# Encoder step on one core: expert dots placed earlier, one-hots shared with ScalarE, later weights in half-row blocks

## The chip, the cores and the metric

One core of one Trainium2 chip runs the whole program. The metric is the device time of one execution in microseconds (us), the median of several runs. The profile shows one execution; its span is counted from the first to the last recorded instruction. MB are 10^6 bytes unless a size in KB stands beside.

## The reference, cut to what matters

640 tokens of width D = 2048 (four tiles of 128 prompt tokens, one tile of 8 x 16 sample tokens) pass one layer, all in float32:

```python
z = (rmsnorm(x) * (1 + sc1) + sh1) @ w_in            # value, gate, q, k, v
y = concat(conv_module(z), band_attention(q, k, v))  # 1024 + 1024 channels
x = x + g1 * (y @ w_out)
h = rmsnorm(x) * (1 + sc2) + sh2                     # PEER retrieval on h
s = (h @ w_pq) . sub_keys                            # 8 heads x 2 x 128 scores
# per head: top 16 of each half, 256 sums, top 16 of those -> 128 experts a token
act = gelu(einsum('td,ted->te', h, u_experts[eidx])) # the "dots"
x = x + g2 * einsum('te,ted->td', softmax(tv) * act, v_experts[eidx])
return rmsnorm(x) * final_g                          # and the new caches
```

There are 16384 experts of 2048 values each, in `u_experts` and in `v_experts`.

## The kernel before, in words

**Tokens.** Tiles 0 and 1 ("first tiles", X, TX = 2) and tiles 2 to 4 ("later tiles", Y, TY = 3; tile 4 holds the sample tokens) are taken through the dense layers one after the other. The first tiles go first, so that their expert retrieval can run beside the dense layers of the later ones.

**Dots.** Each of the 5 x 128 = 640 steps takes one expert per token. POOL (`gather`, L637 to L640) fetches 128 rows of 8 KB, 1 MB, by an indirect DMA into one of NU = 4 buffers `ux`; VectorE (`step`, L1724) multiplies them with h and sums. Dot n belongs to tile n // 128. Behind a dot VectorE runs one piece of `choose` (L1551), the search for the picks of the head after next, 18 pieces a head. `steps(k)` in the VectorE program places k dots: 112 after the first tiles' queries (L1748), 1.5 a head in the later tiles' attention (L1797, L1800), 28 among the residual additions of w_out (L1813), all others after it (L1818). A waiting dot holds up everything behind it on VectorE.

**Weights.** SP loads them in blocks of 256 columns, all 16 row blocks, 2 MB, so 1 KB rows (`load`, L322, `load_pq`, L383). For the later tiles two of the four slots of R0 are in turn, and each load waits until TensorE has done the block two before it. TensorE takes q and k columns with `project` (L743), v rows with `values_part` (L782), w_out with `project_out` (L871), and w_pq with `key_queries` (L893), whose scores ScalarE copies to `SY`. SP saves them (L497), loads tile 2's again as `Sc` (L499); choices 16 and later read them there. ScalarE's copies of v (`keep_values`, L1094) wait for stores of v, which SP issues (`values_out`, L407) between loads; `k_cache(0)` comes after all of them.

**Attention of the later tiles.** For each of 16 heads VectorE runs `head_mask`, `head_max`, `steps(1)`, `head_norm`, then in odd heads `steps(1)`; TensorE runs `scores` (L949 to L955), `weigh` and `turn_weights`. `scores(h)` waits for the maximum of head h-1.

**V side for the prompt tiles, in two pairs of tiles.** `turn_picks` transposes a tile's indices and weights, ScalarE copies them (`copy_turned`, L1269). `one_hots(n)` (L1639) builds four tokens' one-hot rows of both indices on VectorE in one of four slots: L1648 the second index, L1649 the first times the weight. `scatter_tokens` multiplies them on TensorE (L1029) into a 128 x 128 weight matrix a token, and ScalarE copies it into `W` (`keep_W`, L1276). 64 such groups make a pair. `dense(pair)` (L1033) then streams all of `v_experts` in 128 pieces of 1 MB through TensorE (L1040), 16 matmul records a piece, into all eight banks. The one-hots of a pair are built in one go, `burst` (L1699): the first one when dot 256 is due, with 36 pieces of `choose` between; the second when dot DRAIN * TOPK = 33 * 16 = 528 is due, behind `drain` (L1667), which empties the banks:

```python
if n == DRAIN * TOPK:
    drain()
    burst(64, None)
```

One-hot slots share memory with two of the four slots of the pieces, and `W` with the other two, so no piece arrives during a burst.

**End.** Tile 4's V side is 128 gathered picks, added by L1829. Then `first_pair_out` (tiles 0 and 1), tile 4, and `last_pair_out` run one after another (L1832 to L1838), each with `norm_rows` (L1653); SP stores the rows, and loads x1 of the last pair once the first pair is stored. SP issues `finals` (the first pair's inputs and gates) after piece 84 of the second pair.

**Orders.** Nothing is planned at run time: each engine's program is a fixed list, joined by semaphores.

Of the kernel before, what the change touches and what calls it, by code (L numbers as in the profile page):

```python
# [5 lines left out]
def hybrid_encoder_step(nc, ins, outs):  # L6
# [12 lines left out]
    ALU = mybir.AluOpType  # L19
# [28 lines left out]
    DRAIN = 33  # L48
# [8 lines left out]
    with ctx:  # L57
# [64 lines left out]
        vst = VS[:, 0:1024].rearrange("p (b n) -> p b n", b=4)  # L122
        ost = rb(29696, 2048).rearrange("p (b n) -> p b n", b=2)
# [68 lines left out]
        fin = tk(16)  # L192
        assert ms_at[0] <= 3776 and tk_at[0] <= tk_end and late_at[0] <= 3776
# [47 lines left out]
        s_vsty = [sem(f"later_v_stored_{i}") for i in range(4)]  # L241
# [17 lines left out]
        q_done, q_read, s_s, s_se = sem("q2_done"), sem("q2_read"), sem("key_scores"), sem("key_scores_read")  # L259
        w_q = [sem(f"w_pq_{i}") for i in range(2)]  # L260
# [7 lines left out]
        tr_done, tr_read = sem("picks_turned"), sem("turned_copied")  # L268
        oh_rdy, oh_used, w_read = sem("onehots"), sem("onehots_used"), sem("W_copied")
# [4 lines left out]
        s_h2in, s_Sin = sem("h2_in"), sem("keyscores_in")  # L274
        s_fin, s_fin2, s_x1l = sem("final_in"), sem("final_in_sample"), sem("x1_last_in")
# [45 lines left out]
        def _(sp):  # L321
# [72 lines left out]
            for m in range(12):  # L394
                if m < 2:
                    sp.wait_ge(q_done, 14 + 2 * m)
                elif m < 10:
                    sp.wait_ge(z_done, 40 + 2 * (m - 1))
                else:
                    sp.wait_ge(z_done, 56 + 3 * (m - 9))  # L400
                load("w_in", m % 2, (2 + m // 4) * CC + (m % 4) * BW)
                if 8 <= m < 11:
                    i = m - 4
                    sp.wait_ge(s_oE, i + 1)
                    sp.dma_start(kvo["k", 0][i - 2] if i < 6 else kvo["k", 1], ost[:, i % 2]).then_inc(s_osty[i % 2], 16)

                def values_out(j):  # L407
                    for t in range(TX, T):
                        v = j * TY + t - TX
                        sp.wait_ge(z_free, 2 + 56 + v + 1)  # L410
                        dst = kvo["v", 0][t] if t < TP else kvo["v", 1]
                        sp.dma_start(dst[:, j * BW:(j + 1) * BW], vst[:, v % 4]).then_inc(s_vsty[v % 4], 16)

                if m >= 10:
                    values_out(m - 10)
# [1452 lines left out]
```

## Time and profile before

| | us |
|---|---|
| median of 3 runs | 4321.93 (4309.65 to 4325.44) |
| profiled execution, time | 4329.54 |
| profiled execution, span | 4327.7 |
| TensorE busy | 3614.2 (84%) |
| VectorE busy | 2841.8 (66%) |
| GpSimd (POOL) busy | 1160.0 (27%) |
| ScalarE busy | 337.1 (8%) |
| moved by DMA | 1402.75 MB, mean 324 GB/s |

How to read it: busy is the time in which an instruction was recorded on the engine. PEld is TensorE's weight load, which overlaps the multiplies. PEclk is the clock granted to TensorE as a share of full speed. The DMA share is the mean busy share of 16 DMA engines; it can come out a little over 1. Idle time of an engine costs nothing where another one sets the end.

### The profile page before, as it was taken

The numbers are of one execution on the slowest core, as the hardware profiler recorded it, in microseconds if no ns is written. First come the engines' busy times: TensorE is split into PE (matmuls) and PEld (weight loads), VectorE is DVE, ScalarE is ACT, GpSimd is POOL, SyncE is SP. The second block draws the span as 40 slices with busy tenths as digits, with TensorE's granted clock in tenths as the row PEclk, the third lists the DMA queues.
The fourth block names the chain that finished last, engine by engine and source line by source line (L and its number), as shares of the span: only waits on it lengthen the run. The fifth ranks groups of instructions, "written<-read, shape, count | busy, mean of one in ns | idle before, by whom it ended". The sixth has DMA issues, their size and how long they took to land.

```text
span 4327.7 us, 36032 instructions
## 1 busy us (share of the span) xinstructions
PE 3614.2 (84%) x13071; PEld 2135.0 (49%) x13071; DVE 2841.8 (66%) x5321; ACT 337.1 (8%) x763; POOL 1160.0 (27%) x862
## 2 busy tenths in 40 slices
PE   4699899997887989891689999999526899996995
PEld 0466577875456777550534444444215344442442
DVE  2138861148883755887987766676899766664657
ACT  1100013110001400100200000000002000000000
POOL 1100001015661112564043222222641422222221
PEclk8899999998997999895899999999769999998997
DMA  9977834459997879998189999999972999999996
GB/s 350 206 255 243 261 104 150 151 205 401 398 403 251 278 263 334 342 388 326 40 352 418 421 421 407 422 420 421 387 270 84 421 422 419 419 422 395 421 418 256
DMA packets 406612, 1402.75 MB, mean 324 GB/s; under 512 B 22512, under 2 KB 246456, under 8 KB 268933
## 3 DMA queue, kind: packets, MB, share of 16 engines
q0 software_dynamic: 116784, 831.77, 48.5%
q1 hardware_dynamic: 289088, 564.69, 35.8%
q10 hardware_dynamic: 576, 4.19, 0.2%
q8 instruction: 91, 1.49, 0.1%
q14 instruction: 73, 0.60, 0.0%
HBM read 1370.26 MB, written 31.81 MB: 324 GB/s over the span
## 4 chain that ended last, share of the span: by engine, by line
DMA 45%; PE 28%; DVE 12%; issue 10%; POOL 3%; SPq 1%; ACT 1%; another core or an unknown queue 0%; DVEq 0%; POOLq 0%; ACTq 0%
DMA R<-in_u_experts,MS 28%; PE bank L743 13%; DMA R<-in_v_experts,MS 9%; PE bank L871 6%; DVE R L1649 3%; POOL R L639 3%; PE bank L782 3%; DMA R<-in_w_in 3%; DMA R<-in_w_ada 2%; DVE R L1648 2%; DVE R L1829 2%; PE bank L697 1%; PE bank L674 1%; DVE RB L1435 1%; PE bank L955 1%
## 5 line engine op out<-in xcount | busy, mean ns | idle before, releaser
L639 POOL DMA_INDIRECT R<-in_u_experts,MS x640 | 979.7, 1531 | 1859.8 <-DVE MS L1724 1568.7
L1724 DVE CUSTOM_DVE_ANT_0 R<-R 128x2048 f32<-128x2048 f32 x384 | 880.8, 2294 | 406.8 <-DMA R<-in_u_experts,MS 386.7
L1040 PE MATMUL bank<-R,RB 128*128 128x512 f32 x2304 | 1019.0, 600 | 73.4 <-DMA R<-in_v_experts 73.2
L743 PE MATMUL bank<-RB,R 128*128 128x256 f32 (+1 forms) x3072 | 862.8, 443 | 96.4 <-DMA R<-in_w_pq 45.0
L1040 PE MATMUL bank<-RB 128*128 128x512 f32 x1792 | 778.2, 592 | 0.0
L743 PEld LDWEIGHTS bank<-RB,R 128*128 128x128 f32 x3072 | 593.8, 195 | 351.8 <-issue 51.5
L1040 PEld LDWEIGHTS bank<-R,RB 128*128 128x128 f32 x2304 | 440.0, 192 | 642.4 <-issue 544.6
L1724 DVE CUSTOM_DVE_ANT_0 R<-R,RB 128x2048 f32<-128x2048 f32 x256 | 585.9, 2289 | 123.8 <-DMA R<-in_u_experts,MS 122.3
L1040 PEld LDWEIGHTS bank<-RB 128*128 128x128 f32 x1792 | 340.5, 190 | 428.6 <-issue 428.6
L1829 DVE SCALAR_TENSOR_TENSOR R<-R,MS 128x2048 f32<-128x2048 f32 x128 | 301.5, 2355 | 211.1 <-DMA R<-in_v_experts,MS 210.6
L871 PE MATMUL bank<-R,RB 128*128 128x256 f32 x1280 | 279.7, 382 | 10.4 <-DMA R<-in_w_out 9.3
L871 PEld LDWEIGHTS bank<-R,RB 128*128 128x128 f32 x1280 | 244.9, 192 | 44.8 <-DMA R<-in_w_out 9.7
L639 POOL DMA_INDIRECT R<-in_v_experts,MS x128 | 130.8, 1022 | 392.0 <-DVE R L1829 362.8
L1029 PE MATMUL bank<-R 128*128 128x128 f32 x1024 | 164.1, 309 | 83.7 <-DVE R L1649 83.3
L674 PE MATMUL bank<-MS,RB 128*128 128x128 f32 (+4 forms) x497 | 83.4, 320 | 176.8 <-DVE RB L1637 92.3
L1029 PEld LDWEIGHTS bank<-R 128*128 128x128 f32 x1024 | 138.9, 211 | 109.3 <-DVE R L1649 109.0
L1649 DVE TENSOR_SCALAR R<-MS 128x128 f32<-128x128 f32 x512 | 176.3, 344 | 0.0
L1435 DVE SCALAR_TENSOR_TENSOR RB<-RB,MS 128x512 f32<-128x512 f32 x240 | 175.8, 732 | 0.0
L674 PEld LDWEIGHTS bank<-MS,RB 128*128 128x128 f32 (+4 forms) x497 | 66.3, 173 | 190.7 <-DVE RB L1637 92.9
L782 PE MATMUL bank<-R,RB 128*128 128x256 f32 x640 | 142.9, 386 | 14.1 <-DMA R<-in_w_in 10.3
L1354 DVE TENSOR_TENSOR RB<-bank,RB 9x256 f32<-9x256 f32 x128 | 53.5, 418 | 153.3 <-PE bank L697 149.3
L1648 DVE TENSOR_SCALAR R<-MS 128x128 f32<-128x128 f32 x512 | 145.1, 283 | 1.6 <-ACT MS L1269 1.5
(282 smaller groups left out, 1912.9 us busy)
## 6 DMA issues: line engine op xcount, KB each, us to landing
R<-in_v_experts SPq DMA_DIRECT2D x144, 1024.0 KB, 9.1
RB<-in_v_experts SPq DMA_DIRECT2D x112, 1024.0 KB, 9.1
R<-in_w_ada SPq DMA_DIRECT2D x48, 2048.0 KB, 13.2
R<-in_w_in SPq DMA_DIRECT2D x32, 2048.0 KB, 18.5
R<-in_w_out SPq DMA_DIRECT2D x16, 2048.0 KB, 9.2
R<-in_w_pq SPq DMA_DIRECT2D x16, 2048.0 KB, 21.4
R<-in_u_experts,MS POOLq DMA_INDIRECT x640, 10.9
RB<-in_x_prompt POOLq DMA_DIRECT2D x6, 1024.0 KB, 16.6
```

The lines of the kernel that those rows point to most:

```text
L639: pool.indirect_dma_start(dst, None, table, bass.IndirectOffsetOnAxis(ap=expert[T_ % 2][:, c:c + 1], axis=0)).then_inc(signal, 16)
L674: return pe.transpose(out, in_, ident[0:k, 0:k])
L743: m = pe.matmul(PB[2 * par + i][:, 0:src.shape[-1]], w, src[:, k], start=(k == 0), stop=(k == KT - 1))
L782: m_ = pe.matmul(PB[2 * (n % 2)][:, 0:BW], src[:, k, t * P:(t + 1) * P], ring[:, j, k, :], start=(k == 0), stop=(k == KT - 1))
L871: m = pe.matmul(PB[v % 4][:, 0:BW], src[:, k, t * P:(t + 1) * P], ring[:, j % 2, k, :], start=(k == 0), stop=(k == KT - 1))
L1029: m = pe.matmul(PB[n % 4][:, k * P:(k + 1) * P], oneh[n % 4][:, 1, k], oneh[n % 4][:, 0, k], start=True, stop=True)
L1040: x = pe.matmul(PB[4 * h + q][:, :], W[:, i, h * P:(h + 1) * P], vring[slot][:, q * PW:(q + 1) * PW], start=(i == 0), stop=(i == NKEY - 1))
L1435: ch.mark(STT(out=oP, in0=iP, scalar=w, in1=oP, op0=ALU.mult, op1=ALU.add))
L1648: TS(oneh[n % 4][:, 1, k], iota_row, turned[t % 2][:, 1, c:c + 1], None, ALU.is_equal)
L1649: m = TS(oneh[n % 4][:, 0, k], iota_row, turned[t % 2][:, 0, c:c + 1], turned[t % 2][:, 2, c:c + 1], ALU.is_equal, ALU.mult)
L1724: V.tensor_tensor_reduce(u, u, x1[t] if t < TX else h2c, 1.0, 0.0, ALU.mult, ALU.add, dots[t % 2][:, h * TOPK + s:h * TOPK + s + 1]).then_ ...
L1829: STT(out=acc, in0=ux[p % NU], scalar=weight[TP][:, p:p + 1], in1=acc, op0=ALU.mult, op1=ALU.add).then_inc(v_used, 1)
```

## The change

- More dots early: `steps(124)` for 112, three dots a head for 1.5, four after each of twelve w_out residuals.
- The later tiles' w_in, w_out and w_pq come in half-row blocks: 8 of 16 row blocks and 512 columns, 2 MB again, 2 KB rows; sums over both halves stay open in several banks. v and w_out rows are taken 512 columns at a time, v through two staging buffers of 512. The k-cache load moves up.
- ScalarE builds the second index's one-hots of odd groups (distance to the index by Abs, then Relu of 1 minus it).
- DRAIN becomes dot 492. The third tile's groups are built between dots 494 to 511, the fourth tile's in one go when dot 512 is due; ScalarE's program is put in that order.
- The first pair's output runs in nine parts behind V picks 80 to 88; the last rows' squares move to ScalarE.

```diff
-    DRAIN = 33
+    DRAIN = 492
@@ SP
+            def load_half(n, name, at, signal):
+                if n >= 2:
+                    if n % 2 == 0:
+                        sp.wait_ge(y_used, n // 2)
+                    else:
+                        second_half_used(n // 2 - 1)
+                sp.dma_start(wide[:, n % 2], wv[name][:, (n % 2) * 8:(n % 2) * 8 + 8, at:at + PW]).then_inc(signal[n % 2], 16)
...
+            for n in range(12):
+                if n < 2:
+                    sp.wait_ge(q_done, 14 + 2 * n)
+                load_half(n, "w_in", (2 + n // 4) * CC + (n // 2 % 2) * PW, w_in_s)
+                if n == 1:
+                    k_cache(0)
...
+            values_out(0)
+            for n in range(12, 14):
+                load_half(n, "w_out", 0, w_in_s)
+            values_out(1)
...
@@ TensorE
+            for b in range(4):
+                for half in range(2):
+                    weights_in(half)
+                    for c in range(4):
+                        n = 40 + 4 * b + c
+                        if half == 0:
+                            pe.wait_ge(z_free, n - 1)
+                        m = half_columns(hTY, half, c, c)
+                        if half:
+                            m.then_inc(z_done, 1)
+                        elif c == 3:
+                            m.then_inc(y_used, 1)
...
                     pe.wait_ge(oh_rdy, n + 1)
+                    if n % 2:
+                        pe.wait_ge(oh_act, n // 2 + 1)
...
-                for t in (2 * pair, 2 * pair + 1):
-                    turn_picks(t)
-                for t in (2 * pair, 2 * pair + 1):
-                    scatter_tokens(t)
+                turn_picks(2 * pair)
+                if pair == 0:
+                    turn_picks(1)
+                scatter_tokens(2 * pair)
+                if pair:
+                    turn_picks(3)
+                scatter_tokens(2 * pair + 1)
                 dense(pair)
@@ ScalarE
+            for v in range(2 * TY):
+                act.wait_ge(z_done, 56 + v + 1)
+                if v >= 2:
+                    act.wait_ge(s_vsty[v % 2], 16 * (v // 2))
+                A(vstY[:, v % 2], PB[v][:, :], ACT.Copy).then_inc(z_free, 1)
...
+            def distances(n):
+                t, q = divmod(n, P // 4)
+                for k in range(4):
+                    m = A(oneh[n % 4][:, 1, k], iota_row, ACT.Abs, scale=-1.0, bias=turned[t % 2][:, 1, 4 * q + k:4 * q + k + 1])
+                m.then_inc(oh_abs, 1)
+
+            def second_rows(n):
+                act.wait_ge(oh_abs, n // 2 + 1)
+                A(oneh[n % 4][:, 1], oneh[n % 4][:, 1], ACT.Relu, scale=-1.0, bias=ones).then_inc(oh_act, 1)
+
             def keep_W(t):
...
+                for n in range(n0, n1):
+                    at = (t % 2) * P + 4 * (n - n0)
+                    ahead = n % 2 == 0 and n + 3 < n1
+                    if ahead:
+                        if n:
+                            act.wait_ge(oh_used, n)
+                        distances(n + 3)
                     act.wait_ge(oh_used, n + 1)
                     A(W[:, :, at:at + 4], PB[n % 4][:, :].rearrange("p (t i) -> p i t", t=4), ACT.Copy).then_inc(w_read, 1)
+                    if ahead:
+                        second_rows(n + 3)
...
+            def last_squares(n, x, junk, at):
+                act.wait_ge(f_x, n + 1)
+                A(junk, x, ACT.Square, accum_out=fin[:, at:at + 1]).then_inc(s_sq, 1)
...
+            row_sqrt(0, 0, 2)
+            last_squares(0, x1r[2], acc, 10)
+            last_squares(1, x1r[0], accd[0], 0)
+            last_squares(2, x1r[1], accd[1], 1)
+            row_sqrt(1, 10, 1)
+            row_sqrt(2, 0, 2)
@@ VectorE
-                    TS(oneh[n % 4][:, 1, k], iota_row, turned[t % 2][:, 1, c:c + 1], None, ALU.is_equal)
+                    if n % 2 == 0:
+                        TS(oneh[n % 4][:, 1, k], iota_row, turned[t % 2][:, 1, c:c + 1], None, ALU.is_equal)
...
-                if n == DRAIN * TOPK:
+                if n == DRAIN:
                     drain()
-                    burst(64, None)
+                if n == TP * P:
+                    for k in range(4):
+                        weigh_picks(3, k)
+                    for q in range(P // 4):
+                        one_hots(3 * (P // 4) + q)
...
+                if DRAIN + 2 <= n < TP * P:
+                    per = TP * P - DRAIN - 2
+                    m = n - DRAIN - 2
+                    for q in range(m * 32 // per, (m + 1) * 32 // per):
+                        one_hots(2 * (P // 4) + q)
...
-            steps(112)
+            steps(124)
...
                 steps(1)
                 head_norm(h)
-                if h % 2:
-                    steps(1)
+                steps(2)
...
-            for v in range(8 * TY):
+            for v in range(4 * TY):
...
+                steps(4)
...
+                if 80 <= p < 89:
+                    first_pair_out(p - 80)
+
+            last_rows()
```

`last_rows` does tile 4's and the last pair's additions, then the three row scales and outputs; `row_scale` is the small middle part of the old `norm_rows`.

## Rows read from the trace of the kernel before

**Rows 1.** Stretches: length, busy PE, PEld, DVE, ACT, POOL, then PEclk, DMA share, GB/s.

```profile
945.00:1752.00 807.00, 682.32 (x3091) 530.37 (x3089) 548.63 (x1068) 107.26 (x290) 298.24 (x165) 0.89 0.90 329
1388.00:1542.00 154.00, 146.91 (x946) 115.81 (x946) 113.63 (x337) 64.95 (x190) 23.01 (x24) 0.84 0.76 253
1752.00:1955.00 203.00, 183.86 (x608) 111.69 (x608) 170.08 (x267) 15.53 (x32) 135.79 (x64) 0.95 0.99 383
2048.00:2181.00 133.00, 89.29 (x515) 75.58 (x515) 132.97 (x595) 38.70 (x65) 3.82 (x4) 0.85 0.11 41
2181.00:3085.00 904.00, 886.73 (x2047) 389.54 (x2048) 635.66 (x1027) 6.06 (x7) 262.18 (x230) 0.99 1.01 416
3085.00:3207.00 122.00, 0.61 (x2) 0.00 (x0) 111.66 (x184) 0.31 (x1) 98.01 (x42) 0.52 0.95 363
3207.00:3332.00 125.00, 77.20 (x518) 64.94 (x518) 123.45 (x525) 39.33 (x67) 1.55 (x2) 0.95 0.14 49
3332.00:4273.00 941.00, 887.05 (x2037) 389.04 (x2038) 596.01 (x552) 4.00 (x5) 261.59 (x236) 0.97 1.01 414
4273.00:4328.00 55.00, 4.92 (x12) 1.90 (x10) 48.40 (x49) 0.61 (x3) 0.00 (x0) 0.58 0.33 133
```

**Rows 2.** The same view for line 1724 alone; two records are one dot.

```profile
1388.00:1542.00 154.00, 55.05 (x48) 0.84 0.76 253
2181.00:3085.00 904.00, 529.48 (x459) 0.99 1.01 416
3085.00:3207.00 122.00, 94.22 (x84) 0.52 0.95 363
```

**Rows 3.** Timeline of VectorE at the first head and the first w_out residual.

```profile
1387.69 0.29 DVE L1765 CUSTOM_DVE_ANT_0 RB<-bank,MS 128x128 f32<-128x128 f32 x1 [8.14 <-PE bank L955]
...
1562.78 0.42 DVE L1509 TENSOR_TENSOR MS<-bank,RB 128x256 f32<-128x256 f32 x1 [31.62 <-DMA RB<-mod_scratch]
```

**Rows 4.** DMA view of 1026 to 1320 us (three rows), then of 0 to 80.

```profile
q0 software_dynamic: 12712, 92.61, 77.3%
q1 hardware_dynamic: 23942, 25.40, 25.5%
...
R<-in_w_in SPq DMA_DIRECT2D x12, 2048.0 KB, 27.5
...
q1 hardware_dynamic: 9639, 19.46, 72.7%
```

**Rows 5.** Timeline of SP's queue after the later queries.

```profile
1955.61 1.70 SPq L497 DMA_DIRECT2D keyscore_scratch<-RB  x3
1978.22 0.32 SPq L499 DMA_DIRECT2D R<-keyscore_scratch  x1
```

**Rows 6.** Timeline in the bursts, one group of TensorE in each, builds on VectorE.

```profile
2054.84 2.07 PE L1029 MATMUL bank<-R 128*128 128x128 f32 x8 [0.25 <-DVE R L1649]
...
3222.83 0.28 DVE L1648 TENSOR_SCALAR R<-MS 128x128 f32<-128x128 f32 x1
...
3222.97 1.16 PE L1029 MATMUL bank<-R 128*128 128x128 f32 x8 [0.65 <-DVE R L1649]
3223.02 0.34 DVE L1649 TENSOR_SCALAR R<-MS 128x128 f32<-128x128 f32 x1
3223.28 0.28 DVE L1648 TENSOR_SCALAR R<-MS 128x128 f32<-128x128 f32 x1
```

**Rows 7.** ScalarE's groups by form: busy us and mean ns, then the idle time.

```profile
L1276 ACT ACTIVATE RB<-bank 128x512 f32<-128x512 f32 x128 | 76.1, 597 | 171.9 <-PE bank L1029 165.1 <-DMA acc_scratch<-RB 6.8
...
L1246 ACT ACTIVATE RB<-RB,MS 128x512 f32<-128x512 f32 x16 | 11.4, 712 | 0.0
...
L1142 ACT ACTIVATE RB<-RB,MS 128x128 f32<-128x128 f32 x16 | 6.4, 400 | 12.0 <-DVE MS L1488 12.0
...
L1219 ACT ACTIVATE RB<-bank 128x128 f32<-128x128 f32 x16 | 4.6, 285 | 0.0
```

**Rows 8.** Timeline of VectorE at the last output rows.

```profile
4318.60 4.62 DVE L1665 SCALAR_TENSOR_TENSOR RB<-RB,MS 128x2048 f32<-128x2048 f32 x2
```

More of the change, by code:

```diff
@@ L192, in hybrid_encoder_step @@
         fin = tk(16)
+        ones = fin[:, 15:16]
         assert ms_at[0] <= 3776 and tk_at[0] <= tk_end and late_at[0] <= 3776
@@ L391, in _ @@
                 load_pq(m)
[L394 to L415, printed above, removed]
-            values_out(2)
-            values_out(3)
-            for j in range(2):
-                sp.wait_ge(z_done, 56 + 3 * (j + 3))
-                load("w_out", j, j * BW)
             def k_cache(hp):
@@ L434, in values @@
                         sp.wait_ge(s_vst[i], 16 * 2)
+                    for i in range(2):
                         sp.wait_ge(s_vsty[i], 16 * 3)
@@ L466, in _ @@
             sp.dma_start(n2Y, rows(ins["norm2_g"].tensor, [[0, P]], D)).then_inc(s_n2, 16)
-            for j in range(2, 8):
-                sp.wait_ge(o_done, 16 + 3 * (j - 1))
-                load("w_out", j % 2, j * BW)
-                if j == 4:
+            for n in range(14, 20):
+                load_half(n, "w_out", (n - 12) // 2 * PW, w_in_s)
+                if n == 16:
                     sp.wait_ge(s_A2, 3)
@@ L665, in _ @@
             pool.wait_ge(s_osty[1], 16)
-            for i in range(4):
+            for i in range(2):
                 pool.wait_ge(s_vsty[i], 16 * 3)
@@ L921, in _, with half_columns, half_rows @@
             pe.wait_ge(s_se, 16)
-            columns(40, hTY, 8)
+            def half_columns(src, half, c, bank):
+                for i in range(8):
+                    m = pe.matmul(PB[bank][:, 0:NY], wide[:, half, i, c * P:(c + 1) * P], src[:, 8 * half + i],
+                                  start=(half + i == 0), stop=(half + i == 8))
+                return m
+            def half_rows(src, half, t, bank):
+                for i in range(8):
+                    m = pe.matmul(PB[bank][:, :], src[:, 8 * half + i, t * P:(t + 1) * P], wide[:, half, i, :],
+                                  start=(half + i == 0), stop=(half + i == 8))
+                return m
+            for b in range(4):
[10 more added lines that the diff above has]
+                            m.then_inc(y_used, 1)
             for i in range(4, 7):
@@ L1011, in _ @@
             pe.wait_ge(s_h2E, 4 * T)
-            key_queries(1, h2TY, TY)
+            for b in range(4):
+                for half in range(2):
+                    pe.wait_ge(w_q[half], 16 * (4 + b + 1))
+                    for c in range(4):
+                        n = 4 * b + c
+                        if half == 0 and n >= 4:
+                            pe.wait_ge(q_read, 16 + n - 3)
+                        m = half_columns(h2TY, half, c, c)
+                        if half:
+                            m.then_inc(q_done, 1)
+                            if n >= 1:
+                                key_scores(1, n - 1, TY)
+                        elif c == 3:
+                            m.then_inc(y_used, 1)
+            key_scores(1, 15, TY)
             def turn_picks(t):
```

193 lines of the change are left out of this document (118 added, 75 removed).

## The prediction

> **What bounds the kernel now.** I read the windows view first, to cut the span into stretches, then the groups by form and the releasers. [rows 1] show four kinds of stretch. While the later tiles (2 to 4) are projected, 945 to 1752 us, the DMA share averages 0.90 and VectorE is busy 549 of 807 us: dots (L1724) fill gaps between other work. In the two dense stretches, 2181 to 3085 and 3332 to 4273, TensorE (887 of 904 us, 887 of 941) and the DMA engines (1.01) are both full. Between them TensorE has nothing to multiply for 122 us (0.61 us busy) while VectorE runs on to dot 528, where the old DRAIN lies. And in both one-hot bursts, 2048 to 2181 and 3207 to 3332, DMA falls to 0.11 and 0.14 while VectorE is full. The last 55 us are VectorE alone. So the reader should see two things to gain: expert rows moved while a queue is idle, and VectorE time in bursts and tail.
>
> The chip moves 1 MB (1.05 MB decimal) for a dot, a V pick and a dense piece alike. The second dense stretch has 112 dots, 128 picks and 128 pieces in 941 us: 2.56 us each. With free queues a dot costs VectorE 2.9 us, choice included (84 records are 42 dots in 122 us [rows 2]; busy 94.2/42 = 2.24 is the dot, 0.66 the choice).
>
> **Step 1, more dots early (56).** Before, 112 + 24 + 28 = 164 dots are done ahead of the later query projection; after, 124 + 48 + 48 = 220.
> - First projections: 12 dots x 2.9 = 35 us on VectorE after 1326, so it is free for the heads at 1361. Before, it then waited until 1387.7 for the first maximum [rows 3]; the k-cache load is now issued earlier, and the first head needs some 7 us of TensorE. Start 1375: -13. The six later v tiles have banks of their own, but only two staging buffers; v 5's copy waits for v 3's store, which SP issues behind the last w_out load: some 20 us, under the same 35.
> - Heads: before, VectorE did 1.5 dots a head, TensorE 147 of 154 us. Its other work is 113.6 - 55.1 - 24 x 0.66 = 43 us, 2.7 a head. After: 2.7 + 3 x 2.9 = 11.4 us, with its gaps 12.2, times 16 = 195 against 154: +41. VectorE, not TensorE, becomes the bound.
> - w_out: TensorE work is unchanged. VectorE starts 21 us late, waiting for g1 [rows 3], then 12 x (4 x 2.9 + 1.4) + 4.5 = 161 us, then norms and turn, 23 us: from 1575 this chain gives 1780.
> - DMA sets a later end: 807 x 0.90 = 726 share-us are needed already; 56 x 1.05 MB at 0.411 MB a us (416 GB/s by 1.01) add 143, so 945 + 869 = 1814, or 1805 at the share of 1.01 of the dense stretches. I take 1812 for the key queries' start, against 1752: **+60**.
>
> **Step 2, half-row blocks.** They change rows from 1 to 2 KB. In the w_in stretch the 1 KB rows moved 25.40 MB in 25.5% of 294 us, 339 GB/s of their own time; the 2 KB rows of w_ada moved 19.46 MB in 72.7% of 80 us, 335 [rows 4]. So no queue time is gained: 0, bounded by -18 us if 58 MB ran as fast as the gathers (92.6 MB in 77.3%: 407) and 0. What may change is who waits: w_in lands after a median 27.5 us [rows 4] against 20.8 us of TensorE a block. The DMA total above is unchanged by that. On SP the k-cache load (0.5 MB, 1 us of queue time) now stands behind the second half-block, and each half waits for its own half of TensorE's work, 20.5 us before its successor is needed; POOL's queue only loses two waits at its end.
>
> **Step 3, key queries and first burst.** Only 36 dots remain (before 92), done by about 1812 - 10 + 105 = 1907. The queries need TensorE 184 us [rows 1], 203 with their waits. With the gathers gone half way I take 190: 2002. Before, this was hidden under dots; now the burst waits for it. Then the key scores are saved (1955.6 to 1978.2 before, under gathers [rows 5]) and reloaded before choice 16 can run. Bounds 14 (alone) and 32 us (as before); the queues are idle, so 17: 2019.
> ScalarE takes second one-hots of odd groups. A VectorE pair of builds is 0.45 us [rows 6], a group 4 x 0.455 = 1.81, now 1.05 in odd ones: a pair of groups 3.63 -> 2.86. The old burst was 133 us = 64 x 1.81 + 17 (36 choices, handshake); the new 32 x 2.86 + 17 = 108. ScalarE's pair is four Abs, a Relu and two copies. Nearest rows [rows 7]: 0.285 us for 128 columns from a bank, 0.400 for an Exp with sum between buffers, 0.597 for a 512-column copy. So 4 x 0.285 + 3 x 0.597 = 2.93, at most 4 x 0.400 + 3 x 0.712 = 3.74; I take 3.0 because neither new operation sums. It hides in 108/32 = 3.4; at 3.74 the burst is 120. Dense starts at 2127 against 2181: **-54**.
> The Trainium skill (ScalarE: Activation LUTs, Rules for kernel authors) advises VectorE for such operations and budgets about 0.3 us an ACTIVATE plus 0.83 ns an element; that gives 4 x 0.41 + 3 x 0.72 = 3.8 us, the burst 122, a sum 20 us worse with the second one. The trace's 0.285 and 0.597 us are below it, so it stays out of the sum.
>
> **Step 4, first dense stretch.** TensorE's 904 us stay. In them 459/2 = 229 dots ran; after 256 that reaches 485. DRAIN at 492 needs 7 more, 20 us, in place of 122: **-102**.
>
> **Step 5, builds between dots.** Drain 5 us; 20 dots x 2.9 = 58; 32 builds, 16 x 2.86 = 46; handshakes with gelu and the turn 6; the other 32 builds 46 + 3. Sum 164 against 125: **+39**. TensorE's 1.16 us a group and ScalarE's 3 a pair hide in 5.8 us a pair here. POOL was busy 98 us for 42 gathers in [rows 1], 2.3 each, against some 5.4 a step now; that hides too.
>
> **Step 6, second dense stretch.** 128 dots instead of 112: 16 x 2.56 = **+41**. The nine parts of the first pair's output, 2.3 us each, stand beside picks, an operation of the form and size of the last output rows (2.3 us each [rows 8]), that come every 4 us or so: 2.56 us a MB, shared with the pieces: 9 x (4.6 - 4.0) = 5 us late, part made up: **+4**. Its loads are issued at piece 84, some 250 us before pick 80.
>
> **Step 7, tail.** Of 55 us, the first pair took 20 (two each of four 2.3 us operations and the scale). Left: 4.6 sample, 9.6 for eight drains and two adds, 2.5 waiting for ScalarE's squares and root behind them, 3.2 scales, 7 outputs, 4.5 store [rows 8] = 31: **-24**.
>
> Sum: -54 - 102 + 39 + 41 + 4 - 24 = -96 us (the +60 lies inside the -54). The profiled execution had a span of 4327.7 and took 4329.5; it gives 4233. It stands 0.18% over the median 4321.9, so I forecast 4225.
>
> **Rivals.**
> *A, more is gained.* Each weight load lands within the 20.8 us of a block instead of 27.5, so TensorE no longer waits: key start 1800 (-12), queries 180 (-10), the scores' trip 14 (-3), no lag at the picks (-4): 4196. For it: 1 KB rows get only a quarter of the queue time beside the gathers. Against: what they gain the dots lose. The Trainium skill (DMA: Bandwidth & Descriptors, Queues, rings and completion order) says that an engine takes turns between queues packet by packet, so longer rows could raise their share; no row here decides it.
> *B, little is gained.* The early dots cost full price and collide: key start 1845 (+33), the scores' trip 32 (+15), ScalarE at 3.74 in both bursts (+12 + 11): 4296. For it: the queues are 0.90 full before the key queries already, and 0.76 among the heads.
> *C, slower: ScalarE and TensorE in turns.* keep_W runs Abs, waits for a group, copies, runs Relu, and the next copy waits again. If nothing overlaps, a pair is 1.6 + 2.07 + 0.6 + 0.7 + 2.07 + 0.6 = 7.6 us (2.07: a group of TensorE at its lower clock, 1.16 at the higher [rows 6]). First burst 243 (+135), third tile's builds 122 (+73), second's +18: 4451. It decides from 5.4 us a pair: over the 3.4 that VectorE leaves, 48 pairs then cost 96, the whole gain (5.9 us: 0.5% slower). Against it: distances are made three groups ahead, with four slots.
>
> **How the numbers follow.** Forecast 0.60; A 0.15; B 0.17; C 0.08. The forecast's own bounds are +-35 us (burst 12, trip 15, key start 15, lag 10). The range runs from 4150, below A for the 18 us of step 2 and step 1's unsure overlap, to 4305, above B; it leaves out C and edges. About 0.5%, 22 us, is what a measurement of this kernel can tell. Faster by more: forecast, A and half of B, 0.83; same: half of B, 0.09; slower: C, 0.08.
>
> **What would show it.** Right: the first query matmul for later tiles near 1812 with the heads 195 us long; over 70 us without dots ahead of the first burst, which is about 108 long with ScalarE at 3.0 us a pair; dense from 2127; TensorE without dense pieces for 184 us instead of 247 between the dense stretches; no first-pair work after the last pick. Wrong: w_in waits gone and a key start before 1790 (A), dots spaced over 3.3 us after 1326 (B), or VectorE waiting for TensorE in every build (C).

## Result and profile after

The changed kernel takes 4225.9 us, median of 4 runs (4220.1 to 4230.9), against 4319.3 for the kernel before (4 runs): a ratio of 0.978, 95% interval 0.9765 to 0.9797. The forecast was 4225. The profiled execution has a span of 4223.9 us, 104 less than 4327.7; the sum in the prediction gave 96 less. A second set of runs, on the chip of e10 to e12, gave 0.975 (0.9734 to 0.9771). So a difference of some 0.3%, 12 us, between experiments from different sets can be noise in what follows. One run of e3 (6147 us) and one of e9 (9608 us) lie far above all others and are left out of the medians.

The page after, in its rows on DMA and totals (40 equal slices):

```profile
DMA  9977834459999999993199999999948999999996
...
DMA packets 377072, 1402.68 MB, mean 332 GB/s; under 512 B 22416, under 2 KB 187480, under 8 KB 239397
```

The windows view of the changed kernel; columns and stretches as in [rows 1], with the heads as the second row and the later key queries as the third:

```profile
945.00:1792.00 847.00, 697.40 (x2489) 427.81 (x2488) 690.54 (x1276) 103.81 (x279) 387.40 (x220) 0.86 1.00 381
1373.00:1565.00 192.00, 174.33 (x954) 134.53 (x953) 177.66 (x442) 65.01 (x190) 73.55 (x48) 0.72 0.98 354
1792.00:1982.00 190.00, 183.04 (x619) 112.21 (x617) 67.00 (x68) 18.68 (x37) 55.66 (x29) 0.97 0.61 235
2007.00:2112.00 105.00, 74.75 (x508) 65.10 (x506) 105.00 (x463) 91.82 (x223) 3.76 (x4) 0.95 0.12 42
2116.00:3024.00 908.00, 887.53 (x2048) 389.30 (x2047) 640.55 (x1036) 4.78 (x6) 265.94 (x233) 0.99 1.01 417
3031.00:3190.00 159.00, 94.32 (x518) 84.45 (x518) 152.86 (x488) 95.39 (x229) 23.61 (x22) 0.71 0.50 177
3190.00:4131.00 941.00, 888.11 (x2048) 389.94 (x2048) 610.65 (x617) 3.69 (x6) 278.96 (x236) 0.98 1.01 415
4194.00:4224.00 30.00, 0.00 (x0) 0.00 (x0) 22.54 (x27) 6.31 (x8) 0.00 (x0) 0.50 0.25 105
```

Read it beside [rows 1]. The stretch of the later tiles has gone from a DMA share of 0.90 to 1.00: the early dots do fill the queues. But the key queries, where the share was 0.99, now show 0.61, and VectorE is busy for only 67 of their 190 us. The two dense stretches are what they were (TensorE 887 and 888 us busy, share 1.01). The ledger against before is:

| place | before | after | change of its length | forecast |
|---|---|---|---|---|
| start to first dense piece | 2181.2 | 2115.8 | -65 | -54 |
| first dense piece to drain | 1026.2 | 915.0 | -111 | -102 |
| drain to second dense piece | 124.8 | 159.8 | +35 | +39 |
| second dense piece to last pick's end | 940.6 | 1003.2 | +63 | +45 |
| tail | 54.6 | 30.1 | -25 | -24 |

Every stretch lies within 18 us of its forecast, and the sum within 8. In the second profile of the changed kernel (e13) the first dense piece comes at 2126.5 and not at 2115.8, so the first row is good to some 10 us. Where its 65 us come from is another matter. VectorE stands still in the middle of the key queries; its timeline around dot 248, and under it SP's:

```profile
1878.61 2.29 DVE L1850 CUSTOM_DVE_ANT_0 R<-R,RB 128x2048 f32<-128x2048 f32 x1 [0.96 <-DMA R<-in_u_experts,MS]
...
1982.90 0.29 DVE L1740 TENSOR_REDUCE MS<-RB 128x8 f32<-128x128 f32 x1 [101.99 <-ACT RB L1342]
```

```profile
1981.19 1.53 SPq L511 DMA_DIRECT2D keyscore_scratch<-RB  x3
1991.83 0.32 SPq L513 DMA_DIRECT2D R<-keyscore_scratch  x1
```

L1740 is the softmax sum of tile 0's gate, put behind dot 248. It waits for ScalarE's exponential (L1342), and that stands in ScalarE's program behind all 32 copies of the later queries and scores, the last of which ends at 1981.2. Before the change dot 248 came after the queries, so the same order cost nothing. This wait of 102 us was in no step of the prediction. The last seven dots, 249 to 255, ran behind it, beside the save and reload of the scores. Four of them had their rows waiting; the other three needed gathers that POOL could issue only from 1986 on. The burst began at 2006.7.

### The profile page after: what moved, and what is told of

Same layout as the page of the kernel before. It is cut to its first block, busy times and chain, and to the rows that moved or that the text cites. A ratio compares the mean times of both kernels' runs of the same rounds, so it can differ in the third digit from the quotient of the medians.

```text
span 4223.9 us, 34888 instructions
## 1 busy us (share of the span) xinstructions
PE 3631.7 (86%) x12495; PEld 2046.3 (48%) x12495; DVE 2777.5 (66%) x5036; ACT 450.4 (11%) x1083; POOL 1112.4 (26%) x862
## 4 chain that ended last, share of the span: by engine, by line
DMA 47%; PE 25%; DVE 14%; issue 11%; POOL 2%; ACT 1%; another core or an unknown queue 0%; SPq 0%; DVEq 0%; POOLq 0%; ACTq 0%
DMA R<-in_u_experts,MS 32%; PE bank L757 9%; DMA R<-in_v_experts,MS 9%; DVE R L1760 3%; PE bank L939 3%; PE bank L946 3%; PE bank L885 3%; DMA R<-in_w_ada 2%; DVE R L1850 2%; DVE R L1962 2%; POOL R L653 2%; PE bank L796 1%; DMA R<-in_w_out 1%; PE bank L711 1%; DMA R<-in_w_pq 1%
## 5 line engine op out<-in xcount | busy, mean ns | idle before, releaser
L653 POOL DMA_INDIRECT R<-in_u_experts,MS x640 | 899.9, 1406 | 1867.3 <-DVE MS L1850 1534.6
L1112 PE MATMUL bank<-R,RB 128*128 128x512 f32 x2304 | 1015.6, 598 | 77.3 <-DMA R<-in_v_experts 77.3
L1112 PEld LDWEIGHTS bank<-R,RB 128*128 128x128 f32 x2304 | 438.9, 192 | 643.9 <-issue 547.5
L757 PE MATMUL bank<-RB,R 128*128 128x256 f32 (+1 forms) x2048 | 513.4, 412 | 51.1 <-DMA R<-in_w_pq 25.7
L939 PE MATMUL bank<-RB,R 128*128 128x384 f32 x1024 | 338.5, 491 | 15.3 <-DMA R<-in_w_in 9.7
L946 PE MATMUL bank<-R,RB 128*128 128x512 f32 x576 | 258.1, 610 | 24.9 <-DMA R<-in_w_in 13.1
L653 POOL DMA_INDIRECT R<-in_v_experts,MS x128 | 163.1, 1274 | 355.9 <-DVE R L1962 325.4
L1101 PEld LDWEIGHTS bank<-R 128*128 128x128 f32 x1024 | 149.6, 227 | 104.9 <-DVE R L1760 102.4
L946 PEld LDWEIGHTS bank<-R,RB 128*128 128x128 f32 x576 | 112.1, 196 | 169.5 <-issue 139.5
L1760 DVE TENSOR_SCALAR R<-MS 128x128 f32<-128x128 f32 x512 | 154.2, 337 | 0.0
```

The lines of the kernel that those rows point to most:

```text
L653: pool.indirect_dma_start(dst, None, table, bass.IndirectOffsetOnAxis(ap=expert[T_ % 2][:, c:c + 1], axis=0)).then_inc(signal, 16)
L757: m = pe.matmul(PB[2 * par + i][:, 0:src.shape[-1]], w, src[:, k], start=(k == 0), stop=(k == KT - 1))
L939: m = pe.matmul(PB[bank][:, 0:NY], wide[:, half, i, c * P:(c + 1) * P], src[:, 8 * half + i], start=(half + i == 0), stop=(half + i == 8))
L946: m = pe.matmul(PB[bank][:, :], src[:, 8 * half + i, t * P:(t + 1) * P], wide[:, half, i, :], start=(half + i == 0), stop=(half + i == 8))
L1101: m = pe.matmul(PB[n % 4][:, k * P:(k + 1) * P], oneh[n % 4][:, 1, k], oneh[n % 4][:, 0, k], start=True, stop=True)
L1112: x = pe.matmul(PB[4 * h + q][:, :], W[:, i, h * P:(h + 1) * P], vring[slot][:, q * PW:(q + 1) * PW], start=(i == 0), stop=(i == NKEY - 1))
```

## Experiments

Ratios are to the kernel before, run on the same chip; 0.001 is 4.3 us. The last three columns are from the profiled execution of each.

| kernel | median us | ratio (95%) | dot 255 starts | dot 256, behind the burst | dot 256 to the end |
|---|---|---|---|---|---|
| before | 4319 | 1 | 2044.8 | 2178.6 | 2149 |
| changed | 4225.9 | 0.9781 (0.9765 to 0.9797) | 2003.1 | 2111.8 | 2112 |
| changed again (e13) | 4218.5 | 0.9753 (0.9734 to 0.9771) | 2013.9 | 2122.6 | 2105 |
| e3, 164 early dots | 4222.7 | 0.9780 (0.9757 to 0.9803) | 2002.5 | 2111.2 | 2110 |
| e4, one-hots on VectorE | 4271.7 | 0.9900 (0.9876 to 0.9923) | 2007.2 | 2141.1 | 2128 |
| e5, drain at 528 | 4236.1 | 0.9814 (0.9797 to 0.9832) | 1996.7 | 2105.4 | 2112 |
| e6, first pair last | 4241.9 | 0.9829 (0.9804 to 0.9854) | 2003.7 | 2112.4 | 2127 |
| e7, no half rows | 4253.4 | 0.9860 (0.9840 to 0.9880) | 2041.1 | 2149.5 | 2105 |
| e10, 1 KB rows | 4249.6 | 0.9841 (0.9820 to 0.9861) | 2034.5 | 2143.2 | 2102 |
| e11, k cache late | 4229.8 | 0.9787 (0.9771 to 0.9803) | 2007.3 | 2115.9 | 2103 |
| e12, half rows alone | 4287.7 | 0.9920 (0.9904 to 0.9937) | 1998.0 | 2131.8 | 2149 |
| e1, exponential ahead | 4214.5 | 0.9766 (0.9749 to 0.9783) | 1915.2 | 2108.3 | 2104 |
| e2, and choices later | 4202.5 | 0.9738 (0.9720 to 0.9756) | 1912.2 | 2097.7 | 2105 |
| e9, and 200 early dots | 4177.2 | 0.9684 (0.9659 to 0.9709) | 1947.2 | 2072.4 | 2107 |

Nine of these profiles have the program of the changed kernel from dot 256 on (all but before, e4, e5, e6 and e12). Their last column lies between 2102 and 2112 us, 2106 on average: that is how well one profile can be read there. e12, which has the program of before there, repeats its 2149.

### e3: the early dots undone

```diff
-            steps(124)
+            steps(112)
...
-                steps(2)
+                if h % 2:
+                    steps(1)
...
-                steps(4)
+                steps(3 if v % 3 == 1 else 2)
```

> The changed kernel with the counts of early dots as before: 112 after the first picks, 1.5 a head, 28 among the output-projection residuals, 164 ahead of the later key queries in place of 220. Theory (step 1 and 3 as predicted, early dots move work into queues that are partly free, and what they cost there is less than what they save behind): the heads take about 154 us again, the key queries start near 1752 in place of 1792, but 92 dots are left, and they end near 2048 as before; the first burst stays 105 long, so the first dense piece comes near 2155 in place of 2116, and the time is 4226 + 40 = 4266. Rival (the 102 us for which VectorE stood still in front of dot 248 show that the early dots only moved a wait): the first dense piece within 8 us of 2116, and 4226 within 8.

Measured 0.9780, beside 0.9781 and 0.9753 for the changed kernel: nothing lost, or 12 us against the second set, where my own theory had 40. Groups of the later key queries' copies on ScalarE and of the dots beside them (first and last start):

```profile
L1270 ACT ACTIVATE MS<-bank x16: 491/491/493, 1744.5 to 1901.2; 128x384 f32<-128x384 f32 x16
```

```profile
L1850 DVE CUSTOM_DVE_ANT_0 R<-R,RB x256: 2266/2292/2357, 951.4 to 2002.5; 128x2048 f32<-128x2048 f32 x128
```

With 164 early dots the key queries start 79 us sooner (first copy 1744.5 against 1823.5) and have ended at 1903; the dots run on to 2004.8, and the burst starts there, at the same time as in the changed kernel, where the queries' end, the gate's exponential and the seven dots behind it set it. 56 dots were moved and the last one did not move.

### e7, e10, e11, e12: what the half-row blocks bring

e7 takes the half rows out (blocks of 256 columns and the k-cache load as before, with `steps(2)` behind each of the 24 residuals); e12 adds them to the kernel before and nothing else. e10 keeps the blocks and halves the rows; e11 moves one load.

```diff
# e10
-                sp.dma_start(wide[:, n % 2], wv[name][:, (n % 2) * 8:(n % 2) * 8 + 8, at:at + PW]).then_inc(signal[n % 2], 16)
+                rows8 = wv[name][:, (n % 2) * 8:(n % 2) * 8 + 8]
+                sp.dma_start(wide[:, n % 2, :, 0:BW], rows8[:, :, at:at + BW]).then_inc(lo_in[n % 2], 16)
+                sp.dma_start(wide[:, n % 2, :, BW:PW], rows8[:, :, at + BW:at + PW]).then_inc(signal[n % 2], 16)
# e11
-                if n == 1:
-                    k_cache(0)
...
             sp.wait_ge(z_done, 62)
+            k_cache(0)
```

> The changed kernel without the half-row blocks: later weights in blocks of 256 columns (1 KB rows) as before, with 220 early dots, ScalarE's one-hots, the drain at 492 and the first pair among the picks kept. Theory (step 2: the longer rows gain no queue time, and who waits for whom changes little): within 10 us of 4226. Rival (the half-rows halve the waits of TensorE for weights, and are what let the key queries start near 1792 and not 1812, and end 22 us earlier): the first key query of the later tiles at 1810 or after, the first dense piece 15 to 30 us later, 4241 to 4256.

> The changed kernel with each half-row block loaded by two transfers of 1 KB rows (1 MB each) instead of one of 2 KB rows; blocks, banks, order and the early k-cache load are kept. Theory (of the 28 us that e7 lost, 17.6 are TensorE's wait for the k cache, and the rest the rows: 325 GB/s of own queue time with 1 KB rows against 349, and 22 us of queue time over the stretch): the first dense piece 15 to 22 us after 2116: 4226 + 18 = 4244. Rival (rows of either size cost the queues the same, as predicted before the change; what helped was the order of loads and banks): within 5 of 4226.

> The changed kernel with the first k-cache load issued where it was, behind the last value copies, instead of behind the second half-row block. Theory: TensorE waits 17 us for it again and the heads start 10 to 17 us later; the stretch behind is partly limited by the queues, so that 6 to 12 us of it reach the first dense piece: 4226 + 9 = 4235. Rival (VectorE is not at the heads before 1370 in any case, so that the wait is covered): within 3 of 4226.

> The kernel of before with nothing changed but the half-row blocks and what belongs to them (banks, the early k-cache load, two staging buffers); 164 early dots as before. Theory (e3 against before: the dots end at 2005 in place of 2048, with the same early dots): the first dense piece at 2138 in place of 2181, and the time of before less 43: 4278. Rival (the gain of the half rows is there only together with more early dots, which load the queues more): within 12 of before, 4308 or more.

> The changed kernel as it is, on the chip of e10 to e12, so that these have it beside them: 4226 within 5.

e7 loses 0.8 to 1.1% (0.9860 against 0.9781 and 0.9753) and e10 alone 0.6 to 0.9%. The last dot of e10 starts at 2034.5, 21 and 31 us after those of the two profiles of the changed kernel, and e7's at 2041.1. So the size of the rows carries most of it; the 8 us between e10 and e7 by the ratios are within the intervals. e10 also has twice as many transfers, of half the size, but e7, with 1 KB rows in transfers of 2 MB, shows the same rate. The reason stands in the DMA view of 1050 to 1300 us, q1 being the queue of the weights: before, then changed, then e10:

```profile
q1 hardware_dynamic: 20462, 21.54, 25.5%
```

```profile
q1 hardware_dynamic: 12824, 25.01, 26.5%
```

```profile
q1 hardware_dynamic: 20372, 20.72, 24.6%
```

Bytes by share of the 250 us: 338 GB/s of the queue's own time with 1 KB rows, 377 with 2 KB, 337 with 1 KB again. (e7, 1 KB: 339; the other ten profiles with 2 KB rows: 367 to 378. The gathers stay at 406 to 411 in all of them.) In the key queries, where few gathers are left, both are slower, and the step between them stays: 347 and 342 GB/s in the two profiles of the changed kernel, 316 in e10 and 324 in e7. The 28 later blocks are 58.7 MB: at the rates beside gathers 174 us of queue time become 156, or up to 160. The Trainium skill (DMA: Bandwidth & Descriptors, Specifications) puts full rate at 512 B and more. Here 1 KB rows beside gathers are some 10% below 2 KB ones, and the measurement decides.

How far this moves the work is best read from the first matmul of the later key queries, by TensorE's timeline in the changed kernel and in e7:

```profile
1795.00 33.62 PE L939 MATMUL bank<-RB,R 128*128 128x384 f32 x96 [0.69 <-ACT RB L1256]
```

```profile
1831.25 20.91 PE L746 MATMUL bank<-RB,R 128*128 128x384 f32 x64 [0.69 <-ACT RB L1189]
```

With the other profiles this makes a table of both changes to that stretch:

| first key-query matmul, us | 256-column blocks, 1 KB rows | half-row blocks, 2 KB rows |
|---|---|---|
| 164 early dots | 1752.5 (before) | 1714.3 (e12), 1716.3 (e3) |
| 220 early dots | 1831.3 (e7) | 1795.0 (changed), 1806.4 (e13) |

The half rows bring 25 to 38 us in either row. e10, with 1 KB rows in half-row blocks, lies between, at 1820.3. The 56 early dots cost 79 us in the first column and 79 to 92 in the second. From 945 us to this matmul e7 has a DMA share of 0.98 over 886 us, the changed kernel 1.00 over 850: 868 share-us against 850. So about half of the 36 us between them is less queue time, and the other half is time in which the queues of e7 stood free. TensorE's waits for weights and for the k cache in e7, 945 to 2010 us:

```profile
PE bank L746 <- DMA R<-in_w_pq: 36.3, 4, 14.2
PE bank L746 <- DMA R<-in_w_in: 27.7, 6, 6.5
PE bank L874 <- DMA R<-in_w_out: 19.6, 2, 11.3
PE bank L677 <- DMA RB<-in_cache_attn_k: 17.8, 1, 17.8
```

and its waits for weights in the changed kernel:

```profile
PE bank L757 <- DMA R<-in_w_pq: 25.7, 3, 14.8
PE bank L946 <- DMA R<-in_w_in: 13.1, 3, 6.8
PE bank L946 <- DMA R<-in_w_out: 11.1, 3, 5.0
PE bank L939 <- DMA R<-in_w_in: 9.7, 6, 3.4
PE bank L939 <- DMA R<-in_w_pq: 4.9, 2, 3.6
```

The k-cache wait is a tempting line. In e11 it is back, and longer,

```profile
PE bank L687 <- DMA RB<-in_cache_attn_k: 40.7, 1, 40.7
```

yet the first head's maximum comes at 1381.0, between 1374.7 and 1387.0 of the two profiles of the changed kernel, and so do dots 255 and 256. VectorE, with 12 more dots, is not free sooner: that cover the prediction had right. The runs are less sharp: 4229.8 is 4 us above the first set of the changed kernel and 11 above the second, beside which it ran (0.9787 against 0.9753, with intervals that just touch). A cost is not shown, and one up to the theory's 9 is not excluded.

e12 gains 0.8%, 32 us against the median beside which it ran (4320.0). Its profiled execution, the shortest of its runs, has the first dense piece 47 us sooner. The expectation, 43 us, is a little above the interval of the runs (27 to 41); the rival's 12 or less is out. The half rows need no early dots to pay.

### e4: ScalarE's one-hots undone

```diff
-                    if n % 2 == 0:
+                    if True:
                         TS(oneh[n % 4][:, 1, k], iota_row, turned[t % 2][:, 1, c:c + 1], None, ALU.is_equal)
```

and neither `distances` nor `second_rows` in `keep_W`.

> The changed kernel with all one-hots built on VectorE; ScalarE only copies banks. Theory (VectorE sets the length of every build, 1.81 us a group against 1.43): first burst 105 + 28 = 133, builds between dots +12, the fourth tile's builds 45 + 12 = 57: 4226 + 52 = 4278. Rival (ScalarE and the turns of the banks with TensorE set it by now, at 2.8 of the 2.84 us a pair of groups, so that taking ScalarE out gives back much of it): first burst at most 10 longer, and no more than +18 in all: 4244 or less.

Measured 46 us by the medians and 51 by the ratios (0.9900 against 0.9781; 63 against the second set): the theory's 52, and far above the rival's 18. First starts and last starts of the builds, changed and then e4:

```profile
L1760 DVE TENSOR_SCALAR R<-MS x256: 319/334/465, 2006.9 to 2111.6; 128x128 f32<-128x128 f32 x128
```

```profile
L1746 DVE TENSOR_SCALAR R<-MS x256: 327/330/487, 2011.0 to 2140.8; 128x128 f32<-128x128 f32 x128
```

105 us against 130, and between the dense stretches TensorE is without pieces for 193 us against 167. So both places pay: 25 us in the first burst, and 22 behind dot 256 (2128 against 2106). The groups of the changed kernel between 2020 and 2105 us (by form: busy us, mean ns, idle time before) show what sets the pace:

```profile
L1760 DVE TENSOR_SCALAR R<-MS 128x128 f32<-128x128 f32 x208 | 62.7, 336 | 0.0
L1101 PE MATMUL bank<-R 128*128 128x128 f32 x416 | 59.7, 293 | 26.1 <-DVE R L1760 26.1
...
L1355 ACT ACTIVATE R<-MS 128x128 f32<-128x128 f32 x103 | 32.6, 392 | 0.0
L1377 ACT ACTIVATE RB<-bank 128x512 f32<-128x512 f32 x52 | 30.9, 594 | 10.6 <-PE bank L1101 10.2
L1759 DVE TENSOR_SCALAR R<-MS 128x128 f32<-128x128 f32 x104 | 28.5, 274 | 0.0
L1360 ACT ACTIVATE R<-R,MS 128x512 f32<-128x512 f32 x26 | 18.5, 713 | 0.0
```

VectorE never waits. ScalarE's three groups sum to 82.0 us, but their records overlap: it stands idle for 10.6 of the 85 us, so it works 74, 2.9 us for each of the 26 pairs against the 3.0 I took. One more operation of 0.4 us a pair would use up what it has left. The ACTIVATE of 128 columns counts 392 ns as a mean, with overlap; four in a row take 1.27 us in the timeline.

### e5: drain and builds back at dot 528

```diff
-    DRAIN = 492
+    DRAIN = 528
...
                 if n == DRAIN:
                     drain()
-                if n == TP * P:
-                    for k in range(4):
-                        weigh_picks(3, k)
-                    for q in range(P // 4):
-                        one_hots(3 * (P // 4) + q)
+                    for q in range(64):
+                        one_hots(64 + q)
...
```

without the builds between dots, and with ScalarE and TensorE in the order of before.

> The changed kernel with the drain and the builds of tiles 2 and 3 back at dot 528 in one go (ScalarE's share of them kept). Theory (VectorE is the bound of the whole stretch between the two dense ones, so where the drain lies and whether builds stand between dots or behind them changes no sum): 16 dots more ahead of the second dense stretch, 16 x 2.9 = 46, and 16 fewer beside it, 16 x 2.56 = 41, handshakes as they are: 4226 + 5 = 4231, at most +12. Rival (the earlier drain and the builds between dots carry a large part of the gain, since TensorE's wait for the drain, 122 us, is what they removed): +25 or more, 4251 and above.

10 us by the medians, 14 by the ratios (7 to 22 by e5's own interval), but 26 against the second set of the changed kernel: the runs alone fit the theory's 5 to 12 and do not shut out the rival's 25. The profile, which is of e5's shortest run, decides more: from dot 256 to the end it takes 2112 us against 2106, 6 us more, which is the theory's size and within the spread there. In it the last dense piece of the first pair ends at 3013.1 and the next one starts here:

```profile
3236.19 9.25 PE L1112 MATMUL bank<-R,RB 128*128 128x512 f32 x21 [2.22 <-DMA R<-in_v_experts]
```

TensorE is without pieces for 223 us, 56 more than in the changed kernel (3023.6 to 3190.6), and the second dense stretch up to the last pick is 951 us, 53 less. Of the forecast's -102, +39 and +41 the sum, -22, is what counts, and nearly all of it is ScalarE's: e4 loses 22 us behind dot 256.

### e6: the first pair's output behind the picks

```diff
-                if 80 <= p < 89:
-                    first_pair_out(p - 80)
+            for k in range(9):
+                first_pair_out(k)
```

> The changed kernel with the nine parts of the first pair's output behind the last pick instead of among picks 80 to 88. Theory (steps 6 and 7): the tail is 20 us longer, 50 in place of 30, and the picks end 5 us sooner: 4226 + 15 = 4241. Rival (the picks that the parts delay are never made up, so they cost among the picks what they save behind them): the last pick ends 15 us or more sooner, and the time stays within 5 of 4226.

Measured 16 us by the medians, 20 by the ratios (33 against the second set), and 21 behind dot 256 (2127 against 2106). VectorE's timeline from the last pick:

```profile
4182.20 4.61 DVE L1789 TENSOR_TENSOR RB<-RB 128x2048 f32<-128x2048 f32 x2
4186.85 4.62 DVE L1791 TENSOR_TENSOR RB<-RB 128x2048 f32<-128x2048 f32 x2
...
4204.57 2.29 DVE L1804 TENSOR_TENSOR RB<-RB,R 128x2048 f32<-128x2048 f32 x1
4213.92 2.48 DVE L1810 TENSOR_TENSOR RB<-bank,RB 128x512 f32<-128x512 f32 x4 [7.06 <-DMA RB<-x_scratch]
```

The tail is 57 us, 27 longer: 20 for the nine parts and 7 for the last pair's rows, which can be loaded only when the first pair's are stored. The last pick ends 11 us sooner, 4 of them because it starts its first one sooner. In the changed kernel picks among the parts come every 4.5 us (4021.43, 4025.89, 4030.36), and some 8 us are not made up.

### e1, e2, e9: the wait behind dot 248

```diff
# e1: ScalarE's program
+            gate_exp(0)
+            gelu(0)
             keep_queries(1, SY, TY)
...
-            gate_exp(0)
             gate_exp(1)
-            gelu(0)
             gelu(1)
# e2: e1, and in first_burst
-                    if n < 36:
-                        choose(2 * NPH + n // 18, n % 18)
+                    if 8 <= n < 44:
+                        choose(2 * NPH + (n - 8) // 18, (n - 8) % 18)
# e9: e2, and
-                steps(2)
+                steps(1 + h % 2)
...
-                steps(4)
+                steps(3)
```

> The changed kernel with ScalarE's exponential and gelu for tile 0 ahead of its copies of the later key queries and scores instead of behind them; nothing is left out. Theory (VectorE stood 102 us in front of the softmax sum behind dot 248 because that exponential stands behind all those copies): the wait goes, the dots end near 1905, and the burst waits for the last scores' save and reload (1982 to about 1996) instead of for 8 dots: it starts near 1996 in place of 2007, the rest is as it was: 4226 - 10 = 4216. Rival (the copies are what ends last in any case, and the last 8 dots only filled the time of the reload): the burst starts within 3 us of 2007, and 4226 stays within 4.

> As e1, and the 36 choices within the first burst stand behind groups 8 to 43 instead of 0 to 35, so that the first builds do not wait for the reloaded scores. Theory (in e1 the burst's first choice waits for the reload): the first builds run near 1992, 4 to 5 us ahead of e1: 4212. Rival (ScalarE's W copies wait for the save of the key scores, whose place they take, and the banks are full after four groups): no more than 2 us to e1, 4216.

> As e2, with 200 early dots in place of 220: 2.5 a head, 3 behind each residual, so that 56 are left beside the key queries, where VectorE stood idle. Theory (each early dot moves the start of the key queries by 0.68 us, 38 us for 56, and the dots left take 3.2 us each): key queries from 1778 in place of 1792, ending near 1968, the dots near 1960: 14 us ahead of e2: 4198. Rival (the key queries slow down with more gathers beside them by what they start earlier): within 4 us of e2, 4212.

VectorE's waits between 1700 and 2110 us, in e1, in e2 and in e9:

```profile
DVE MS L1741 <- ACT RB L1341: 74.0, 1, 74.0
...
DVE MS L1681 <- DMA R<-keyscore_scratch: 9.8, 1, 9.8
```

```profile
DVE MS L1741 <- ACT RB L1341: 71.8, 1, 71.8
```

```profile
DVE R L1851 <- DMA R<-in_u_experts,MS: 54.6, 44, 4.4
DVE MS L1741 <- ACT RB L1341: 11.4, 1, 11.4
```

In e1 the dots are done at 1917, but VectorE then waits 74 us for tile 1's exponential, behind the same copies: the wait has only moved by seven dots, from behind dot 248 to behind dot 255. What the edit is worth is better read from the queries' last copy (L1270) to dot 256, since the queries themselves come up to 10 us apart between profiles of one order. That way is 132.6 us in the changed kernel (1979.2 to 2111.8) and 133.0 in its second profile (1989.6 to 2122.6), 120.6 in e1 (1987.7 to 2108.3), 115.1 in e2 (1982.6 to 2097.7) and 115.2 in e9. So e1 gains 12 there, about the 10 expected, with 9.8 us of the burst spent on the first choice's wait for the reloaded scores; choices eight groups later (e2) take back 5 of these, as expected. In the whole time e1 can't be told from the changed kernel (0.9766 against 0.9781 and 0.9753), and e2 only against one set of its runs.

e9 acts on the real imbalance. In e2, as in the changed kernel, TensorE is late (queries end at 1985) and VectorE early; 20 dots moved back from the heads and residuals make the first copy of the key queries 32 us sooner (1799.5 against 1831.7), the last 25 sooner, and VectorE's wait 11 us. Against e2 the gain is 23 us by the ratios and 25 at dot 256, where I had 14: I took 0.68 us of the queries' start for each early dot, and the 20 dots gave 35 us (first matmul 1770.9 against 1805.6). The first dense piece comes at 2076.3, 40 us sooner than in the changed kernel, and the ratio is 0.9684, outside all other intervals. e9 beats both kernels: 49 us under the changed one by its median, some 30 to 42 by the ratios. It leaves nothing out. With the exponential ahead, 164 early dots were not tried.

## Why the prediction was right, and where it was not

- **Step 1** had the mechanism, and a size too small. VectorE was free at 1370 (1361) and the first maximum came at 1374.7 (1375); the heads took 190 us (195), at a DMA share of 0.98. The key queries' first matmul came at 1795 (1812), but only with the half rows. The step counted none of their effect, so its 1812 is to be held against e7, where it comes at 1831: the 56 early dots cost 79 us and not 60. The sum of queue time was right (869 share-us forecast, 868 in e7); the queues were busy at a share of 0.98 and not of 1.00, which is 17 of the 19 us. In its third point the step named the wrong releaser: VectorE's first residual waited 36 us for TensorE's w_out bank (L946), not 21 for g1.
- **Step 2** failed. "So no queue time is gained: 0" held 1 KB rows beside gathers (339 GB/s) against w_ada's 2 KB rows in a stretch without them (335) [rows 4]. Beside gathers the rate went from 338 to 377 GB/s, 18 us of queue time. That this is the bound I had put is chance: 58 MB at 339 and at 407 GB/s differ by 29 us, not 18. The key queries started 25 to 38 us earlier with the half-row blocks; by e10 the rows are worth 0.6 to 0.9%, by e12 the whole block 0.8%.
- **Step 3**, of -54: 25 for ScalarE, and 29 for the early dots. ScalarE's 25 were right (e4: 105 against 130 us in the burst). The early dots' 29 were wrong: e3 gives 0 (12 against the second set). 19 of them went to the later start of the key queries (step 1). Most of the rest is what the step failed to ask, what else stands behind dots 248 to 255: weigh_picks(0), and through it ScalarE's order; e1 gives 12 back. That these two make up the 29 is arithmetic over separate runs, not an experiment of its own. The queries' end was forecast for 2002 and came at 1981, the burst for 2019 and came at 2007: between them lay 26 us and not 17, seven dots instead of the scores' trip alone.
- **Steps 4 to 6**: 915 us to the drain (924), 160 between (164), 1003 to the last pick's end (986). The extra 17 us are some 8 of picks delayed by the parts (e6), where I had 4, and more time for the same megabytes: the other 995 us for 384 of them are 2.59 each, not 2.56. The sum of the three was forecast at -18 and measured at -13.
- **Step 7**: 30 us (31). ScalarE's squares and root hid as said, 2.1 us of wait.
- **Rivals.** C did not come: ScalarE waits 10 us in 85 and VectorE not at all. B did not, though it had a point in step 1: with 1 KB rows the key queries start at 1831, between 1812 and its 1845, and the half rows hid that. A had a part of the cause, weights that land sooner, but not by a larger share of the engines' time, which stayed between 24 and 27% for the weights' queue: it moved more bytes in that time. The queries took 190 us and not 180, and the score trip was not 14 us but a wait for other reasons; its time, 4196, was too low for this kernel. The undone part e3 would have been a better rival: that the early dots are worth nothing.

So the time was met by two errors of opposite sign: 29 us too much for the early dots, and 32 us or more too little for the half rows. That they cancelled is luck; steps 4 to 7 and ScalarE's part in the burst were met on their merits. By one experiment each the change is: half rows 32 (e12) to 47 (its profile), ScalarE 46 to 51, first pair 16 to 20, the drain's place 10 to 14, early dots 0. The sum, 104 to 132, is over the 93 measured. Parts that share cover would do that, and so would the 12 us between sets; no run here tells them apart.

The Trainium skill's budget (ScalarE: Activation LUTs, Rules for kernel authors) would, as an estimate, have put the burst at 122; it took 105, so leaving it out of the sum was right here.

## What to carry to other kernels

Work moved ahead pays only if everything that stands behind it on each engine can move too: before moving it, list what the moved instructions are queued with, and which engine's program order feeds those. When two engines must both be finished before the next stage, move work until both end together; more moved than that is paid in full and gains nothing. And a queue's rate should be read from a stretch with the same neighbours as the one that is to be changed.

## What the runs showed of the hardware

Beside gathers, 1 KB rows moved at 337 to 339 GB/s of their queue's own time (before, e7, e10) and 2 KB rows at 367 to 378 (the other eleven profiles), in the same 250 us of each. With few gathers beside them, in the key queries, it was 316 and 324 (e10, e7) against 347 and 342 (changed, e13). A TensorE wait of 41 us for one 0.5 MB load (e11) cost nothing that its trace shows, and 11 us at most by the medians. A VectorE wait of 102 us that looked like the bound gave 12 us when it was taken away (e1), because another of 74 us, for the next exponential behind the same copies, took its place: the longest wait of a profile is not its price.
